# Issuing a mixer's 66 small TensorE products between the dense products of its last input group

## The reference, cut to what matters

```
proj = xn @ w_in
k_c, v_c, k_s, v_s, k_w, v_w = kvs          # from proj
def compress(z, pe, w1, w2):
    blk = z[:, idx] + pe[:, None, :]
    hdn = jax.nn.gelu(jnp.einsum('bnlgd,lde->bnge', blk, w1))
    return hdn @ w2
kc = compress(k_c, pe_k, w1_k, w2_k)
vc = compress(v_c, pe_v, w1_v, w2_v)
```

## Time and profile before

| | us |
|---|---|
| median of 3 runs | 2442.07 |
| lowest and highest run | 2436.05, 2443.95 |
| the profiled execution | 2432.06 |
| its span, first to last instruction | 2430.1 |
| the mean granted TensorE clock in it | 0.959 of full |

### The profile page before, as it was taken

One profiled execution on the slowest core, in us unless ns is written; L12 is line 12 of the kernel. 1 busy time (PEld: TensorE's weight loads), 2 busy tenths in 40 slices (PEclk: granted clock), 3 DMA queues, 4 the chain that ended last, 5 costly groups with the idle time before them and its releaser, 6 DMA issues.

```text
span 2430.1 us, 25885 instructions
## 1 busy us (share of the span) xinstructions
PE 2240.5 (92%) x10040; PEld 1681.5 (69%) x10040; DVE 1230.1 (51%) x1672; ACT 925.9 (38%) x1436; POOL 179.7 (7%) x222
## 2 busy tenths in 40 slices
PE   6899999986999977998889999989999988999998
PEld 4667666665666646866778888878755556888887
DVE  5735543256777745345554444443345546444544
ACT  3443531144555524214431134343254454222343
POOL 0240000201000010001000000020222100000000
PEclk9999999998999987999989999999899998999999
DMA  9304123927999973220222322332000002332321
GB/s 362 104 20 139 35 99 121 359 91 259 361 373 381 372 267 107 78 83 13 69 79 87 104 88 103 101 110 87 19 1 1 1 1 69 96 104 87 104 88 69
DMA packets 148459, 309.38 MB, mean 127 GB/s; under 512 B 17774, under 2 KB 19699, under 8 KB 148341
## 3 DMA queue, kind: packets, MB, share of 16 engines
q1 hardware_dynamic: 120468, 229.75, 27.9%
q10 hardware_dynamic: 16500, 36.62, 4.4%
q0 software_dynamic: 11376, 41.42, 4.3%
HBM read 276.56 MB, written 30.99 MB: 127 GB/s over the span
## 4 chain that ended last, share of the span: by engine, by line
PE 78%; DVE 9%; DMA 5%; ACT 4%; issue 3%; POOL 1%; ACTq 0%; POOLq 0%; DVEq 0%; SPq 0%; PEldq 0%
PE PB L1596 52%; PE PB L2040 5%; PE PB L2309 3%; DMA BIG<-in_expert_w_down 3%; PE PB L1581 2%; PE PB L2285 1%; DVE WL L2407 1%; PE PB L1822 1%; PE PB L2111 1%; PE PB L2286 1%; PE PB L2248 1%; DVE X L2467 1%; PE PB L1743 1%; DVE CI L3175 1%; PE PB L1722 1%
## 5 line engine op out<-in xcount | busy, mean ns | idle before, releaser
L2407 DVE TENSOR_TENSOR WL<-RING,WH 128x1024 fp32r<-128x1024 f32 x224 | 277.2, 1238 | 641.9 <-ACT WH L909 391.4
L909 ACT CAST WH<-RING 128x1024 fp32r<-128x1024 f32 x224 | 235.0, 1049 | 833.1 <-PE PB L1596 821.9
L1596 PE MATMUL PB<-HTH,WH 128*128 128x512 f32 x1056 | 416.2, 394 | 13.3 <-DVE WL L2407 9.1
L1596 PE MATMUL PB<-HTL,WH 128*128 128x512 f32 x1056 | 413.7, 392 | 0.0
L1596 PE MATMUL PB<-HTH,WL 128*128 128x512 f32 x1056 | 413.4, 391 | 0.0
L1596 PEld LDWEIGHTS PB<-HTH,WH 128*128 128x128 f32 x1056 | 200.1, 189 | 59.2 <-issue 9.8
L1596 PEld LDWEIGHTS PB<-HTH,WL 128*128 128x128 f32 x1056 | 199.8, 189 | 42.2
L1596 PEld LDWEIGHTS PB<-HTL,WH 128*128 128x128 f32 x1056 | 200.0, 189 | 41.4 <-issue 0.7
L1596 PE MATMUL PB<-WH,NHH 128*128 128x512 f32 x512 | 199.4, 389 | 1.8 <-DVE NHL L2410 1.8
L1596 PE MATMUL PB<-WH,NHL 128*128 128x512 f32 x512 | 199.2, 389 | 0.0
L1596 PE MATMUL PB<-WL,NHH 128*128 128x512 f32 x512 | 199.2, 389 | 0.0
(11 more groups left out here) (514 smaller groups left out, 3522.2 us busy)
## 6 DMA issues: line engine op xcount, KB each, us to landing
RING<-in_mlp_w SPq DMA_DIRECT2D x64, 1024.0 KB, 5.2
RING<-in_expert_w_gate SPq DMA_DIRECT2D x32, 1024.0 KB, 7.5
RING<-in_expert_w_up SPq DMA_DIRECT2D x32, 1024.0 KB, 12.0
BIG<-in_expert_w_down ACTq DMA_DIRECT2D x15, 2048.0 KB
BIG<-in_ada_w SPq DMA_DIRECT2D x10, 2048.0 KB, 11.1
RING<-in_w_in SPq DMA_DIRECT2D x20, 1024.0 KB, 5.1
dispatch_rows<-BIG POOLq DMA_DIRECT2D x24, 512.0 KB, 16.1
RING<-in_a_w_in SPq DMA_DIRECT2D x10, 1024.0 KB, 5.1
```

Of the source, the lines that this page charges most:

```text
L909: ins = nc.scalar.copy(weight_buffers(stage)[0][:, q % 2], halves_of(n, q))
L1596: yield pe.matmul(dst, lhs, rhs, start=(start and n == 0), stop=(stop_ and n == 2))
L2407: ins = V.tensor_tensor(wl, halves_of(n, q), wh.bitcast(F32), ALU.subtract)
```

## The change

On PE the two transposes, the 32 compression products and the 32 position rows' products become 66 steps, and the last group (m = 4) issues six of them after each of its steps b from the third weight part on, but for the very last (n = 2: six places, n = 3: five places; 11 x 6 = 66). The waits move with them. Nothing is left to be issued after the last dense product: `between(len(steps))` finds no step. On DVE the copy into `PET` moves ahead of the last `values_and_low`. ACT, POOL and SP have the same instructions in the same order.

```diff
--- before.py
+++ after.py
@@ -2184,6 +2184,48 @@
                                     stop=(k == ND - 1 and n == 2))
             ins.then_inc(acc_done, 1)
             split_group(g + 3, "cin", 8, "T")
+            steps = []
+
+            def page_rows_T(m):
+
+                if m == 0:
+                    pe.wait_ge(aux_in, AUX["cmp"])
+                    pe.wait_ge(acc_free[0], (g + 4) // 2 + 1)
+                ins = pe.transpose(PB[2][0:DH, m * CMP_LEN:(m + 1) * CMP_LEN], PER[:, m, :], IDENT[0:CMP_LEN, 0:CMP_LEN])
+                if m == 1:
+                    ins.then_inc(c_mm, 1)
+
+            def compress(m, l):
+
+                if l == 0:
+                    pe.wait_ge(zk_moved if m == 0 else zv_moved, 1)
+                z = ZS[m][:, :, 2 * l:2 * l + CMP_STRIDE * (NCMP - 1) + 1:CMP_STRIDE]
+                dst = PB[m][0:DH, 0:NSA_G * NCMP].rearrange("p (a b) -> p a b", a=NSA_G)
+                ins = pe.matmul(dst, CWS[:, m, l, :], z, start=(l == 0), stop=(l == CMP_LEN // 2 - 1))
+                if l == CMP_LEN // 2 - 1:
+                    ins.then_inc(c_mm, 1)
+
+            steps += [lambda m=m: page_rows_T(m) for m in range(2)]
+            steps += [lambda m=m, l=l: compress(m, l) for m in range(2) for l in range(CMP_LEN // 2)]
+
+            def page_bias(m, l):
+
+                if (m, l) == (0, 0):
+                    pe.wait_ge(c_dve, 1)
+                ins = pe.matmul(PB[3][0:DH, m:m + 1], CWS[:, m, l, :], PET[:, m, l:l + 1], start=(l == 0),
+                                stop=(l == CMP_LEN // 2 - 1))
+                if (m, l) == (1, CMP_LEN // 2 - 1):
+                    ins.then_inc(c_mm, 1)
+
+            steps += [lambda m=m, l=l: page_bias(m, l) for m in range(2) for l in range(CMP_LEN // 2)]
+            taken = [0]
+
+            def between(count):
+
+                for step in steps[taken[0]:taken[0] + count]:
+                    step()
+                taken[0] += count
+
             for m in range(3, 5):
 
                 await_set(g + m + 1)
@@ -2209,26 +2251,10 @@
                                     ins.then_inc(part_begun, 1)
                                 if b == 0 and k == 0 and x == 1 and q % 2 == 0:
                                     begin(ins, None)
+                        if m == 4 and n > 1 and (n, b) != (3, 1 + NT):
+                            between(6)
                 ins.then_inc(acc_done, 1)
-
-            pe.wait_ge(aux_in, AUX["cmp"])
-            pe.wait_ge(acc_free[0], (g + 4) // 2 + 1)
-            for m in range(2):
-                ins = pe.transpose(PB[2][0:DH, m * CMP_LEN:(m + 1) * CMP_LEN], PER[:, m, :], IDENT[0:CMP_LEN, 0:CMP_LEN])
-            ins.then_inc(c_mm, 1)
-            for m in range(2):
-                pe.wait_ge(zk_moved if m == 0 else zv_moved, 1)
-                for l in range(CMP_LEN // 2):
-                    z = ZS[m][:, :, 2 * l:2 * l + CMP_STRIDE * (NCMP - 1) + 1:CMP_STRIDE]
-                    dst = PB[m][0:DH, 0:NSA_G * NCMP].rearrange("p (a b) -> p a b", a=NSA_G)
-                    ins = pe.matmul(dst, CWS[:, m, l, :], z, start=(l == 0), stop=(l == CMP_LEN // 2 - 1))
-                ins.then_inc(c_mm, 1)
-            pe.wait_ge(c_dve, 1)
-            for m in range(2):
-                for l in range(CMP_LEN // 2):
-                    ins = pe.matmul(PB[3][0:DH, m:m + 1], CWS[:, m, l, :], PET[:, m, l:l + 1], start=(l == 0),
-                                    stop=(l == CMP_LEN // 2 - 1))
-            ins.then_inc(c_mm, 1)
+            between(len(steps))
 
             def maxima(h, b, turn):
 
@@ -3141,12 +3167,12 @@
             upto(18)
             values_and_low(0, 0)
             upto(20)
-            values_and_low(1, 4)
             dve.wait_ge(c_mm, 1)
             for half in range(2):
                 ins = V.tensor_copy(PET[half * DH:(half + 1) * DH, :, :],
                                     PB[2][0:DH, 0:2 * CMP_LEN].rearrange("p (m l two) -> p m l two", m=2, two=2)[:, :, :, half])
             ins.then_inc(c_dve, 1)
+            values_and_low(1, 4)
             V.memset(SUMS[:, :], 1.0)
             link(V.memset(WT[:, :, :].bitcast(F32), 0.0))
             dve.wait_ge(c_mm, 4)
```

## The result

The changed kernel takes 2447.45 us (median of 8 runs, 2442.87 to 2452.52) where the kernel before takes 2441.48 (8 runs, 2436.05 to 2443.95). The ratio, estimated from the single runs, is 1.0032 (+7.8 us; that of the two medians is 1.0024), with an interval of 1.0017 to 1.0048, so +4.1 to +11.7 us. A second timing of the same pair gave 1.0039 (1.0022 to 1.0055). The profiled execution of after took 2448.53 us, with a span of 2446.6.

The account below looks back on a forecast made before the run. PE was taken as the bound, busy 92% of the span. Inserted products 17.9 plus uncovered wait 9.3 make 27.2 us against 18.47 before, a rise of 8.7 on the 2442.07 median: 2450.8 us, range 2445.5 to 2457.

Parts of the forecast that it names:

- The sign and the mechanism: Whole kernel: slower (0.70), since small products that covered 9 us of bank emptying move away and nothing covers it; rise 8.7 us.
- the wait for `BC`: Behind the last dense product: PE waits for DVE's way to the bias column, 9.3 us, where the wait was 0.5.
- going to and fro between the two kinds, 11 places: Last group on PE: cost of changing between dense and small products, bounds 0 to 1.0 us, taken as 0.5.
- 0.18 + 13.50 + 3.7: Last group on PE: microseconds added by two transposes, 64 compression records and 64 one-column records, at full price.
- First rival: Last group: one-column products' weight loads hide under dense products; rise 5.0 us, 2447.1 us; chance 0.08.
- Second rival: Behind the wait: the clock survives the idle stretch, saving 4.2 us; rise 4.5, 2446.6 us; chance 0.04.
- Third rival: Kernel before: its clock falls only in some executions; rise up to 12.9 us, 2455.0 us; chance 0.12.
- Fourth rival: Last group: the clock falls among the interleaved one-column products, costing 1.7 us or more; 2452.5 to 2460 us; chance 0.08.
- Fifth rival: Last group: the small products hide within the dense group; all hidden gives -9.2 us, 2432.9 us; chance 0.03.
- the 17.9 us: Last group on PE: total time the inserted small products add before the last dense product ends, nothing hidden.

Follow-up runs that it names:

- pos_only: Against the changed kernel: only transposes and position rows' products stay between the dense products, compression products follow the last dense product; 0.9986 of the kernel before.
- comp_only: Against the changed kernel: only transposes and compression products stay between the dense products, position rows' products follow the last dense product; 1.0011 of the kernel before.
- mixed_gates: pos_first_gates with four one-column records after each two of the first 16 compression products; 2435.04 us against 2437.47 for the kernel before, ratio 0.9988.
- filled: The changed kernel plus 21 unused compression products behind the last dense product, to keep PE busy in the wait; 1.0039 of the kernel before.
- places22: The changed kernel with the 66 small products at 22 places of three instead of 11 of six; profiled only, group 37.70 us against 31.81.
- one_place: The changed kernel with all 66 small products at one place, behind the first step of the third weight part; 1.0037 of the kernel before.
- gates_only: The kernel before with ACT starting the 16 gates' transfers ahead of the gelu; 2438.16 us against 2438.13 for the kernel before, ratio 0.9994.
- pos_first_gates: pos_first with ACT starting the 16 gates' transfers ahead of the gelu; 2432.31 us against 2438.44 for the kernel before, ratio 0.9968.
- pos_first: The kernel before with transposes at one place in the last group, then position rows' products before compression products behind the last dense product; 0.9982 of before.
- before_again: The unchanged kernel before, profiled a second time; 31.56 us to the first maxima against 29.87 in its first profile; no timing given.

## Why the prediction was right, and which term was mis-sized

- **The sign and the mechanism held.** PE has no idle time in the last group, the wait for `BC` is the largest of PE in the third mixer at 9.12 us (9.3 predicted), the clock is 0.50 from within it and at the first maxima product, and from there to the compressed keys nothing changed. The median, 2447.45 us, lies within the range; the likeliest value, 2450.8, was 3.4 us above it. Measured as a rise it is 6.0 and 10.2 us in the two timings, where 8.7 was predicted. That the number is so near is in part luck: the stretch itself rose by 11.3 us, or by 9.6 against the second execution of before.
- **The mis-sized term is "going to and fro between the two kinds, 11 places".** I took 0.5 us with bounds of 0 to 1.0; it is 3.3. The one place shown above: the last dense product to the first one-column record takes 0.22 us where two dense ones are 0.11 to 0.12 apart (+0.10); the twelve records 0.78 us where 12 x 0.058 is 0.70 (+0.08); and from the first dense product behind them to the second 0.23 (+0.11). That is 0.29 us per place, and 0.18 + 13.50 + 3.7 + 11 x 0.30 = 20.7 is the 20.69 that the group grew by. The other kernels agree: pos_only's seven places leave (5.90 - 0.2 - 3.7) / 7 = 0.29, comp_only's six (15.57 - 0.2 - 13.5) / 6 = 0.31. The earlier trace rows has only the last of the three, since the transposes there enter free of charge; I read the missing two as absent everywhere. Even so 11 returns at its 0.1 make 1.1 us, above my upper bound. And the earlier trace rows had the entry: the first position rows' transpose starts 1718.06 - 1717.85 = 0.21 us behind the last dense product, where two dense ones are 0.12 apart. Why the experts' transposes enter without it no run here shows; they have 128 weight columns like the dense products, and all the small products here have 64 or fewer. The whole rise in the stretch, 11.3 us against the first execution of before, is 2.6 above the 8.7 for this reason.
- **That the medians rose less than the stretch's 11.3 us** has no cause of its own that I found: over before's second execution the stretch rose by 9.6 (9.2 to the mixer's output), and both timings hold these values.
- **First rival, loads hidden under dense products: false.** Within a place the one-column records are not cheaper than in a row. The rule that I weighed for it says that PE can pull a weight load ahead of a running matmul (the Trainium skill, "TensorE: Matmul & The Clock Gate", section "Step-by-step: what each phase is for"): in mixed_gates four one-column records at half clock take 0.37 us (1726.09 to 1726.46), 93 ns each instead of 107, so at most 14 ns per record are hidden. The trace doesn't contradict the rule, but it was worth nothing in the changed kernel.
- **Second rival, the clock survives: false, and its price too.** It fell 2.9 us into the idle stretch. Where it was held up (filled), nothing was gained up to the compressed keys. The 4.2 us that I had put on it left out that the clock falls at +8.4 to +8.9 us in every kernel that begins the maxima at 1.00.
- **Third rival, before's clock falls only in some executions: half true.** In three of three it was low at the first maxima. What varies is 1.7 us in the one-column products, and it makes before longer, not shorter.
- **Fourth rival, the clock falls in the interleaved stretch: not in the changed kernel (1.00 over 32.00 us), but in places22 and one_place.** It cost 3.2 us in the one and 1.7 in the other.
- **Fifth rival, faster: false.** Nothing of the 17.9 us was hidden; 20.7 were added.
- **A rule that speaks for such a change.** In after PE is the busiest engine in the dense group and idle in the wait behind it. The Trainium skill says in "Perfetto Trace Analysis", section "Optimization Strategy", that a kernel whose most-contended engine changes over time may gain by interleaving those regimes. Its condition was not met before the change: in the dense group and in the block the busiest engine was the same, PE (18.00 us busy of 18.00 and 13.60 of 13.60), so there were no two regimes to interleave. The two that after has came from the change, which took the cover from DVE and ACT.

## What to carry to other kernels

Before work is moved forward on the bound engine, ask what runs on the others beside it where it stands now: comp_only shows 4.76 us of products that cost nothing behind the last dense product and their full price before it. Work put between products of another kind paid for each place here (0.3 us), which speaks for few large lots; the 64 one-column records in one row show the limit of that, since the clock fell behind them. Where two chains end close together (12.35 and 12.01 us), an edit to one can measure as no change (gates_only, filled). Here both together gave 0.3% in pos_first_gates, with the products that feed the other engines first in the cover and ACT's transfers out of the way of its cast; mixed_gates, with both as well and a block 0.85 us longer, can't be told from before.

## What the hardware showed that I had not expected

- Going from the dense products to the small ones and back costs 0.29 to 0.30 us (after); between the two small kinds it costs nothing (mixed_gates). The dense products are split and have 128 weight columns, the small ones are unsplit and have 64: which of the two makes the price no run here separates. The unsplit transposes of 128 columns in the earlier trace rows, which enter free but pay for the return, speak for the columns as to the entry.
- The strided compression records take 0.21 us at either clock. In pos_first most of the keys' records ran at half clock and the values' at the full one, yet both lots took about the same (6.96 and 6.91 us above). The windows of pos_first:
```profile
1727.30:1732.20 4.90, 4.90 (x25) 4.73 (x25) 2.93 (x5) 0.95 (x2) 4.51 (x7) 0.50 0.00 0
1732.40:1740.70 8.30, 8.30 (x41) 5.87 (x39) 0.00 (x0) 1.64 (x2) 6.08 (x8) 1.00 0.00 0
```
  What limits them is thus not TensorE's clock. The Trainium skill says in "SBUF — State Buffer", section "Door 1: The DMA port swizzle (why `[64,N]` ≈ `[32,N]`)", that an access which crosses to a new 16-byte line pays a penalty; the stride of 16 elements does so at each element, which agrees with the rows, though no run here changed the stride, so this cause is not shown.
- The granted clock fell while PE counted as busy all the time: among the 64 one-column records (before, before_again), 0.3 us behind them (one_place), and in the mixture of mixed_gates (then 0.50 with 13.60 us busy of 13.60). Within the maxima it fell too, but there PE had gaps (6.71 of 8.60 us busy in filled). A busy PE in the profile is no sign that the clock will stay up.
